# Expert outputs added up in DRAM by the scatter, and a tail that reads two sums per token instead of eight rows

## The reference

```
h2      = rmsnorm(x1) * (1 + sc2) + sh2
scores  = sigmoid(h2 @ w_router);  idx = top_8(scores + b_router) of 64 experts
wts     = 2.5 * scores[idx] / sum(scores[idx])
routed  = sum over the 8 experts e of a token:
              wts_e * ((silu(h2 @ w_gate_e) * (h2 @ w_up_e)) @ w_down_e)      # 1024 -> 256 -> 1024
shared  = (silu(h2 @ w_gate_s) * (h2 @ w_up_s)) @ w_down_s
x       = x1 + g2 * (routed + shared)
y       = rmsnorm(x, final_norm_w)
```

## Time and profile before

| | |
|---|---|
| median of three runs | 1163.04 us |
| the profiled execution | 1161.44 us |
| its span | 1159.7 us |
| PE busy | 932.3 us (80%) |
| DVE busy | 302.9 us (26%) |
| ACT, POOL busy | 169.5 us, 92.6 us |
| moved by DMA | 308.15 MB |
| expert loop, first gate/up to last scatter | 542 to 1094 us |
| tail behind the last scatter | 1098 us to the end |

### The profile page before, as it was taken

One profiled execution on the slowest core, in us unless ns is written; L12 is line 12 of the kernel. 1 busy time (PEld: TensorE's weight loads), 2 busy tenths in 40 slices (PEclk: granted clock), 3 DMA queues, 4 the chain that ended last, 5 costly groups with the idle time before them and its releaser, 6 DMA issues. The chain is left out here.

```text
span 1159.7 us, 12591 instructions
## 1 busy us (share of the span) xinstructions
PE 932.3 (80%) x4843; PEld 476.4 (41%) x4843; DVE 302.9 (26%) x560; ACT 169.5 (15%) x277; POOL 92.6 (8%) x162
## 2 busy tenths in 40 slices
PE   2699999999966999686999798987879778897500
PEld 0355567865511577433443333422334233332200
DVE  1507630560001321630212121211212112121057
ACT  0212511121000001201111111111111111111100
POOL 1000000000000000000111111211102112111000
PEclk9799999999986999797999998988999989899855
DMA  7822333113379240178699999999999999998390
GB/s 292 271 61 86 107 109 109 37 37 109 103 305 371 73 163 1 55 325 351 259 420 419 422 411 396 410 389 418 395 409 401 388 404 404 405 411 336 113 418 37
DMA packets 77389, 308.15 MB, mean 266 GB/s; under 512 B 10024, under 2 KB 38740, under 8 KB 49040
## 3 DMA queue, kind: packets, MB, share of 16 engines
q1 hardware_dynamic: 63120, 277.36, 60.8%
q0 software_dynamic: 10368, 25.18, 5.6%
q10 hardware_dynamic: 3840, 4.78, 1.2%
HBM read 297.33 MB, written 22.54 MB: 276 GB/s over the span
## 5 line engine op out<-in xcount | busy, mean ns | idle before, releaser
L450 PE MATMUL bank<-arena 128*32 128x512 f32 (+2 forms) x1536 | 277.8, 640 | 51.7 <-issue 50.9
L1393 PE MATMUL bank<-arena 128*128 128x384 f32 x640 | 208.3, 488 | 0.0
L450 PEld LDWEIGHTS bank<-arena 128*32 128x32 f32 (+2 forms) x1536 | 94.1, 131 | 233.0 <-issue 233.0
L1393 PEld LDWEIGHTS bank<-arena 128*128 128x128 f32 x640 | 122.1, 191 | 86.1 <-issue 2.3
L479 PE MATMUL bank<-arena 128*32 128x512 f32 (+2 forms) x768 | 130.9, 596 | 0.6 <-issue 0.6
L464 DVE TENSOR_TENSOR arena<-arena,bank 128x256 f32<-128x256 f32 x36 | 21.6, 599 | 229.7 <-ACT arena L461 229.7
L1378 PE MATMUL bank<-arena 128*2 128x512 f32 x192 | 34.2, 824 | 42.2 <-ACTq L1222 21.4
L479 PEld LDWEIGHTS bank<-arena 128*32 128x32 f32 (+2 forms) x768 | 39.4, 123 | 66.0 <-issue 66.0
L461 ACT ACTIVATE arena<-bank 128x256 f32<-128x256 f32 x36 | 22.1, 615 | 302.7 <-PE bank L450 302.7
L424 POOL DMA_INDIRECT arena<-h_rows,arena x36 | 37.4, 1038 | 314.4 <-DVE arena L418 236.3
L484 DVE TENSOR_SCALAR arena<-bank,arena 128x512 f32<-128x512 f32 x36 | 27.0, 751 | 105.3 <-PE bank L479 105.3
(11 more groups left out here) (228 smaller groups left out, 668.8 us busy)
## 6 DMA issues: line engine op xcount, KB each, us to landing
arena<-in_w_gate_e_dram SPq DMA_DIRECT2D x64, 1024.0 KB, 15.2
arena<-in_w_up_e_dram SPq DMA_DIRECT2D x64, 1024.0 KB, 29.5
arena<-in_w_down_e_dram SPq DMA_DIRECT2D x64, 1024.0 KB, 30.6
arena<-in_w_mod_dram SPq DMA_DIRECT2D x24, 1024.0 KB, 10.4
arena<-in_w_in_dram SPq DMA_DIRECT2D x22, 1024.0 KB, 5.3
arena<-expert_rows SPq DMA_DIRECT2D x3, 4096.0 KB, 21.6
arena<-in_w_out_dram SPq DMA_DIRECT2D x4, 1024.0 KB, 5.9
arena<-in_x_sample_dram ACTq DMA_DIRECT2D x2, 1024.0 KB, 15.6
```

The source lines that it names most:

```text
L450: ins = pe.matmul(bank[off:off + width, :], x_T[:, k, off:off + width], w[:, :, k, :], start=(k == 0), stop=(k == KT - 1))
L1393: ins = pe.matmul(ps[:, 0:TOK], w[:, k, P * (n % 2):P * (n % 2) + P], hT[:, k, :], start=(k == 0), stop=(k == KT - 1))
```

## The change

The scatter no longer writes each result to a row of its own. It adds it to one of two sums per token in DRAM (`expert_sums`, 768 rows of 4 KB, 3 MB): the first expert of a pass adds to sum 0, the second to sum 1, so that no row stands twice within a scatter. The parts:

1. The scatter carries `compute_op=ALU.add` (L433 in the new numbering), and scatter(i) waits until scatter(i-1) has landed. The first one waits for the zeroing.
2. ACT zeroes the sums with one 3 MB store from a zeroed tile (L1274), behind its first activations; DVE waits for it before it overwrites that tile.
3. `vals` has three values instead of four, and the running sums for the rank fall away. The row number in the sums is the token's number plus 0 or 384, by the partition (`far`, made once at the start).
4. In passes 4, 5 and 6 DVE computes `y_shared * g2` and adds it to `x1` (two operations on 128x1024 each).
5. The tail reads 1 MB per tile (two sums). DVE does three operations of 128x1024 per tile instead of six with 128x4096 and 128x2048 among them; the normalization of a tile comes behind the sums of the next one; ACT loads the Sqrt table before the tail.

```diff
-    rows_dram = nc.dram_tensor("expert_rows", [TOK * TOPK, D], F32).ap()
+    sums_dram = nc.dram_tensor("expert_sums", [2 * TOK, D], F32).ap()
...
-        def row_numbers(dve, b):
-            dve.tensor_tensor(rows_i[:, b, :], banks[7][:, 1:3], far, ALU.add)
-            return dve.tensor_copy(wt[:, b:b + 1], banks[7][:, 3:4])
+        def layout_of(quad):
+            return 0 if len(quad) == 1 else 1 if quad[0][2] == 96 else 2
+
+        def row_numbers(dve, b, layout):
+            dve.tensor_tensor(rows_i[:, b, :], banks[7][:, 1:2].to_broadcast([P, 2]), far[:, layout, :], ALU.add)
+            return dve.tensor_copy(wt[:, b:b + 1], banks[7][:, 2:3])
...
         def scatter_rows(pool, x, g, b):
             pool.sem_inc(x["rows_seen"], 1)
-            pool.indirect_dma_start(out=rows_dram,
+            pool.indirect_dma_start(out=sums_dram,
                                     out_offset=bass.IndirectOffsetOnAxis(ap=rows_i[:, g, 1:2], axis=0),
                                     in_=y_e[b], in_offset=None,
-                                    bounds_check=bound["scatter"], oob_is_err=False).then_inc(x["scattered"][b], 16)
+                                    bounds_check=bound["scatter"], oob_is_err=False, compute_op=ALU.add).then_inc(x["scattered"][b], 16)
...
             def scatter(i):
                 pool.wait_ge(x["y_a"], i + 1)
                 pool.wait_ge(x["y_b"], i + 1)
+                if i:
+                    pool.wait_ge(x["scattered"][(i - 1) % 2], 16 * ((i - 1) // 2 + 1))
+                else:
+                    pool.wait_ge(S["acc_zeroed"], 16)
                 scatter_rows(pool, x, i % 4, i % 2)
...
                 weighted_a(dve, i % 2, i % 4).then_inc(x["y_a"], 1)
+                if i in (4, 5, 6):
+                    link(dve.tensor_tensor(y_shared[:, i - 4, :], y_shared[:, i - 4, :], g2_rows[:, SEQ_OF[i - 4], :], ALU.mult))
+                    link(dve.tensor_tensor(x1[:, i - 4, :], x1[:, i - 4, :], y_shared[:, i - 4, :], ALU.add))
...
+                    if h == 0:
+                        dve.wait_ge(S["acc_zeroed"], 16)
...
             for t in range(NT):
-                ins = dve.tensor_tensor_scan(rank[:, t, :], ones[:, 0:NE], chosen[:, t, :], 0.0, ALU.mult, ALU.add)
-            link(ins)
-            link(dve.tensor_tensor(rank, rank, chosen, ALU.subtract))
...
-            for t in range(NT):
-                dve.wait_ge(rows_in_sem[t], 16)
-                r = rows_all[:, t]
-                link(dve.tensor_tensor(r[:, 0:4, :], r[:, 0:4, :], r[:, 4:8, :], ALU.add))
-                link(dve.tensor_tensor(r[:, 0:2, :], r[:, 0:2, :], r[:, 2:4, :], ALU.add))
+            def joined(t):
+                dve.wait_ge(sums_in_sem[t], 16)
+                r = sums_in[:, t]
                 link(dve.tensor_tensor(r[:, 0, :], r[:, 0, :], r[:, 1, :], ALU.add))
-                link(dve.tensor_tensor(r[:, 0, :], r[:, 0, :], y_shared[:, t, :], ALU.add))
                 link(dve.tensor_tensor(r[:, 0, :], r[:, 0, :], g2_rows[:, SEQ_OF[t], :], ALU.mult))
                 link(dve.tensor_tensor(x1[:, t, :], x1[:, t, :], r[:, 0, :], ALU.add))
                 dve.sem_inc(S["routed_ready"], 1)
+
+            def normed(t):
                 dve.wait_ge(S["final_sq"], t + 1)
...
+            for t in range(NT):
+                joined(t)
+                if t:
+                    normed(t - 1)
+            normed(NT - 1)
...
-            full_rows = rows_dram.rearrange("(t p k) d -> t p k d", p=P, k=TOPK)
-            for t in range(NT):
-                sp.dma_start(rows_all[:, t], full_rows[t]).then_inc(rows_in_sem[t], 16)
+            full_sums = sums_dram.rearrange("(m t p) d -> t p m d", m=2, p=P)
+            for t in range(NT):
+                sp.dma_start(sums_in[:, t], full_sums[t]).then_inc(sums_in_sem[t], 16)
...
             act.sem_inc(S["log_ready"], 1)
+            act.dma_start(sums_dram.rearrange("(r p) d -> p r d", p=P),
+                          at(a_st, D).unsqueeze(1).to_broadcast([P, 2 * NT, D])).then_inc(S["acc_zeroed"], 16)
...
+            act.activation(stat2[:, 15:16], ones[:, 0:1], ACT.Sqrt)
             for t in range(NT):
-                act.wait_ge(S["routed_ready"], 2 * t + 1)
+                act.wait_ge(S["routed_ready"], t + 1)
```

More of the change, by code:

```diff
@@ L236, in score_tile @@
             return at(a_x + 3 * NE * n, NT, NE)
-        scores, biased, rest, chosen, rank = (score_tile(n) for n in range(5))
+        scores, biased, rest, chosen = (score_tile(n) for n in range(4))
         top8 = at(a_x + 3 * NE * 5, NT, 8)
@@ L253, in program @@
         mod_rows = at(a_rows, 3, 512)
-        vals = at(a_rows, NT, NE, 4)
+        vals = at(a_rows, NT, NE, 3)
         onehot = at(a_rows + 768, 2, NT, ROWS)
@@ L274, in program @@
         actT_e = at(a_z + 1280, DE)
-        qv = at(a_z + 1536, 2, 2, NT, 4)
+        qv = at(a_z + 1536, 2, 2, NT, 3)
         order_i = at(a_z + 1584, NE).bitcast(I32)
@@ L286, in program @@
         part_f = at(take(1), 1)
-        far = at(take(2), 2)
+        far = at(take(6), 3, 2)
         most_f = at(take(1), 1)
         most_i = at(take(1), 1).bitcast(I32)
-        tok_far = at(take(2 * NT), 2, NT)
+        tok_far = at(take(NT), NT)
         before = arena[:, take(64):top[0]].bitcast(BF16)
@@ L359, in unit_view @@
             return v.rearrange("p (k n) -> p k n", k=KT)
-        rows_all = arena[:, 0:NT * TOPK * D].rearrange("p (t k d) -> p t k d", t=NT, k=TOPK)
-        rows_in_sem = [sem(f"rows_in{t}") for t in range(NT)]
+        sums_in = arena[:, 0:2 * NT * D].rearrange("p (t m d) -> p t m d", t=NT, m=2)
+        sums_in_sem = [sem(f"sums_in{t}") for t in range(NT)]
         ex_names = ("picked onehot_done tab_done rows_ready rows_seen xtr_done xT_a xT_b gu_done sil_done act_done "
@@ L503, in pool_experts @@
             bound["gather"] = pool.to_reg(TOK - 1)
-            bound["scatter"] = pool.to_reg(TOK * TOPK - 1)
+            bound["scatter"] = pool.to_reg(2 * TOK - 1)
             pool.wait_ge(S["order_ready"], 1)
@@ L611, in act_experts, with dve_experts @@
                 weighted_b(act, i % 2, i % 4).then_inc(x["y_b"], 1)
-        def dve_experts(dve, x):
+        def dve_experts(dve, x, link):
             def one_hot(i):
@@ L625, in numbers @@
                     dve.wait_ge(x["scattered"][i % 2], 16 * (i // 2 - 1))
-                row_numbers(dve, i % 4).then_inc(x["rows_ready"], 1)
+                row_numbers(dve, i % 4, layout_of(QUADS[i])).then_inc(x["rows_ready"], 1)
             def x_half(i):
@@ L724, in dve_spill @@
                 dve.wait_ge(x["tab_done"], n + 1)
-                row_numbers(dve, 0).then_inc(x["rows_ready"], 1)
+                row_numbers(dve, 0, 0).then_inc(x["rows_ready"], 1)
                 dve.wait_ge(x["xtr_done"], n + 1)
@@ L751, in vector_part_a @@
             link(dve.tensor_copy(iota1, iota_i))
-            link(dve.memset(far[:, 0:1], FAR))
-            link(dve.memset(far[:, 1:2], TOPK * FAR))
+            link(dve.memset(far.rearrange("p a b -> p (a b)"), FAR))
+            for layout, edge in ((1, 96.0), (2, 64.0)):
+                link(dve.tensor_scalar(far[:, layout, 1:2], part_f, edge, float(TOK), ALU.is_ge, ALU.mult))
+                link(dve.tensor_scalar(far[:, layout, 1:2], far[:, layout, 1:2], FAR, None, ALU.add))
             for t in range(NT):
-                dve.tensor_scalar(tok_far[:, 0, t:t + 1], part_f, float(P * t) - FAR, None, ALU.add)
-                link(dve.tensor_scalar(tok_far[:, 1, t:t + 1], part_f, float(P * t) - FAR, float(TOPK), ALU.add, ALU.mult))
+                link(dve.tensor_scalar(tok_far[:, t:t + 1], part_f, float(P * t) - FAR, None, ALU.add))
             link(dve.tensor_reduce(eye32, ident.rearrange("p (q r) -> p r q", r=32), AX.X, ALU.add))
@@ L1051, in vector_part_b @@
             for t in range(NT):
-                ins = dve.tensor_tensor_scan(rank[:, t, :], ones[:, 0:NE], chosen[:, t, :], 0.0, ALU.mult, ALU.add)
-            link(ins)
-            link(dve.tensor_tensor(rank, rank, chosen, ALU.subtract))
-            for t in range(NT):
-                dve.tensor_scalar(vals[:, t, :, 1], ones[:, 0:NE], tok_far[:, 0, t:t + 1], None, ALU.mult)
-                dve.tensor_scalar(vals[:, t, :, 2], rank[:, t, :], tok_far[:, 1, t:t + 1], None, ALU.add)
-            link(dve.scalar_tensor_tensor(out=vals[:, :, :, 3], in0=scores, scalar=ROUTED_SCALE,
+                dve.tensor_scalar(vals[:, t, :, 1], ones[:, 0:NE], tok_far[:, t:t + 1], None, ALU.mult)
+            link(dve.scalar_tensor_tensor(out=vals[:, :, :, 2], in0=scores, scalar=ROUTED_SCALE,
                                           in1=weight_sum.unsqueeze(2).to_broadcast([P, NT, NE]),
@@ L1110, in vector_part_b @@
                 dve.sem_inc(S["routed_ready"], 1)
+            def normed(t):
                 dve.wait_ge(S["final_sq"], t + 1)
                 link(dve.tensor_scalar(stat[:, t:t + 1], stat2[:, t:t + 1], 1.0 / D, EPS, ALU.mult, ALU.add))
```

(2 more changed lines are left out.)

8 lines of the change are left out of this document (4 added, 4 removed).

## The result

The changed kernel takes 1172.14 us (median of four runs, 1170.93 to 1175.59) against 1162.03 before on the same chip: a ratio of 1.0088, 95% interval 1.0057 to 1.0118. It is slower by 10 us (0.9%). Forecast was 1156, 0.5% faster. The profiled execution took 1171.46 us, its span is 1169.7.

The account below looks back on a forecast made before the run. The prediction took a DVE-bound tail and a DMA-bound middle of the loop as the limits. Its terms, -36.1 + 28 + 1.5 = -6.6 us, gave 1156 us after adjusting to the runs' median, with a range of 1128 to 1196.

Parts of the forecast that it names:

- What bounds the kernel: Whole kernel: a tail that hangs on DVE, and a stretch from 580 to 1060 us bound by DMA bytes.
- The tail, -36.1: From SP's read-back to the end: 61.3 us before, 25.2 after, so 36.1 us saved.
- The scatter's bytes, +28: In the saturated stretch the addition's extra read takes the place of weight bytes, costing 28 us.
- Its first half: At the scatter: an addition has to read the destination too, 12.58 MB more.
- Its price two ways: Extra read in the saturated stretch: 27.5 us by bytes at 407 GB/s, 28.9 us by the queue's share.
- The wait, 0: On POOL, waiting for the scatter before costs 0; its landing was estimated at 11 to 14 us.
- The last scatter, +1.5: At the loop's end the scatter runs alone, 3.6 us before; the added read was taken as 1.5 us.
- What costs nothing: Zeroing store, two DVE operations in passes 4 to 6, dropped running sums: no cost; Sqrt load already in the tail.
- the hidden read: Rival in the saturated stretch: the addition's read is free, 1127 us, or half free, 1142; chance 0.24.
- the chain: Rival in the loop: scatters stand one landing time apart, 67 us more in place of 28, 1195 us; chance 0.14.
- an addition at three times a row's price: Rival at the scatter: the extra is 56 us, time 1184; chance 0.26 together with scatters waiting on each other.
- the total stays: DMA engines move 424 GB/s without scatters, 420 with: a scattered byte takes the place of a weight byte.

Follow-up runs that it names:

- e1: The changed kernel with the addition left out: the scatter overwrites, the wait and zeroing stay. 1127.29 us, ratio 0.9686.
- e2: The changed kernel without the addition, each pass issuing a second plain scatter of the same rows to a second table. 1173.20 us.
- e3: The kernel before, its scatter to 3072 rows of their own adding instead of writing, no wait between scatters. 1205.84 us.
- e8: The kernel before with the filled places dealt out over the groups of partitions that one DMA engine serves. 1146.20 us, ratio 0.9854.
- e7: The changed kernel with the filled places dealt out over the groups of partitions that one DMA engine serves. 1146.40 us, ratio 0.9845.
- e10: The changed kernel with places spread over engine groups and, for one large expert, towards engines that small experts leave free. 1136.18 us, ratio 0.9765.
- e11: The kernel before with the places dealt evenly over groups of 8 neighbouring partitions. 1169.25 us, ratio 1.0051.
- e5: The changed kernel without the addition, plus a direct store of all 128 rows per pass, 18.9 MB in all. 1169.94 us.

## Why the prediction was wrong, by its own steps

- **What bounds the kernel**: right. The tail and the saturated stretch are the two places; e1 separates them.
- **The tail, -36.1**: right, -35.7. The first load landed in 4.8 us (4.9 taken); three operations of 1.24 us a tile, with about 0.1 us more behind each tile; ACT's square lay hidden, since DVE waited only 0.33 us for the root. The store took 3.1.
- **The scatter's bytes, +28**: this is the step that failed. Its first half held: the addition is one more transfer (e1, e2, e3). Its price did not. "Its price two ways" took 11.18 MB by the mean rate and by the queue's mean share, and both ways divide the load evenly over 16 engines. The loop waits for the most loaded one, which has 288 rows where the mean is 192, so 28 has to be taken 288/192 = 1.5 times: 42. Measured are 43.0 at the last scatter's start, of which e1, without the addition, has 1.7 (its last scatter starts at 1095.37), so 41.3 for the addition.
- **The wait, 0**: right. e1 keeps it, and POOL never waited for it. The landing of 10.3 us is below the estimate of 11 to 14.
- **The last scatter, +1.5**: 2.7. A lone adding scatter lands after 6.0 us instead of 3.6 (below).
- **What costs nothing**: right within the 1.7 us of e1. The zeroing store raised the DMA share from 100 to 120 us from 0.34 to 0.70, and PE stayed at 20.00 of 20:

```profile
100.00:120.00 20.00, 20.00 (x64) 11.79 (x63) 19.64 (x19) 0.98 (x2) 0.00 (x0) 1.00 0.70 259
```

- In pass 4 the two new operations of DVE ran at 610.75 and 612.00, and the one-hot behind them at 613.86, ahead of the look-up.
- **The rivals**: the hidden read is out (e1), the chain is out, and an addition at three times a row's price (56 us) is as far from the measured 41.3 as 28 is, and is no mechanism: the addition is two transfers (e2), both dear. The range of 1128 to 1196 held the time, but by its width alone: it reached so far up for a chain that did not come. The side was wrong.

The rows could have shown it. With scatter and gather the rate was 420 in the stretch picked for the earlier trace rows, against 424 without, and from that "the total stays" was read. Over the whole stretch it is 407. The prediction names the missing part as a reason for the hidden read, as time that may be free; all of it but the 4 GB/s between 424 and 420 was the uneven load, which makes a transfer dearer. The 20 us picked lie early in the loop: of the 40 slices on the page of the kernel before, those from 580 to 667 us show 419 to 422 GB/s, and those from there to 1044 us 388 to 418. From 640 to 1040 us, before and then e8:

```profile
640.00:1040.00 400.00, 338.69 (x2116) 141.82 (x2110) 68.66 (x174) 58.47 (x103) 59.98 (x96) 0.94 1.00 404
```

```profile
640.00:1040.00 400.00, 346.31 (x2178) 144.88 (x2171) 70.99 (x180) 59.97 (x105) 61.36 (x99) 0.95 1.02 420
```

With the places spread, the 420 of the early stretch hold to the end of the loop.

All of the extra read shows in the share and none of it in the bytes. The queue of the gathers and scatters, after and then in e1:

```profile
q0 software_dynamic: 10368, 25.19, 8.5%
```

```profile
q0 software_dynamic: 10368, 25.18, 5.8%
```

Packets and MB are the same with and without the addition, but the time of the packets is 8.5% of 1169.7 us, 99 us, instead of 65. One by one: in e1 a packet of 4 KB (one row) takes 159 ns in the median; after, the same 6144 packets fall into two halves, one at 159 and one at 327 ns. So an adding packet takes twice a plain one's time, and the mean of the added time over 16 engines is about the 28 to 33 us that the prediction had; the rest of the 41 is the uneven load.

The Trainium skill, Collectives: The Full Stack, section "The bandwidth ceiling: the fold count and why AG ≠ RS ≠ AR", has the adding step of a ring at half the rate of a copy, because the addition needs two source reads; the runs here agree, 327 ns against 159 for a packet, and e1 and e2 with 44.8 us against 45.9. The Trainium skill, DMA: Bandwidth & Descriptors, section "The descriptor swizzle", gives each engine four neighbouring partitions and the four that lie 32 further for a transfer of 128 partitions. The places of e7 to e10 follow that grouping, and together with e11 they bear it out for indirect transfers too.

## What to carry to other kernels

Where a stream of loads keeps the DMA engines full, price a further transfer by the rows of its most loaded engine, not by its bytes: a gather or scatter whose empty places lie together costs as if they were filled. Spread the filled places over the groups of partitions that one engine serves; here that alone is 17 us of 1163 with no byte less. An addition in DRAM is a second transfer of the same rows: move it into a full stream only if it saves more than that elsewhere, and compare it with mending the part it is meant to shorten.

## What the runs showed of the hardware that was not expected

- **A DMA share of 1.00 does not say that all engines are at work all the time.** It was 1.00 from 580 to 1060 us in before, after, e2, e5 and e8 alike, with rates from 376 to 414 GB/s. The rate beside the best stretch without scatters, 424, says more.
- **The read of an adding transfer is in no count of bytes**, so GB/s falls where nothing got slower but the work per byte.
- **An adding scatter is dearer on GpSimd**: 1.60 us of issue instead of 1.01, and one copy behind it (L403) takes 757 ns in the median, where it takes 200 before and 201 in e1. DVE's one-hot comes later for it, but PE's look-up still starts right behind gate and up (630.09 us in one pass, where gate and up end at 630.16), so it cost nothing here. The rows of e7 and then e8, where all 64 copies stand together:

```profile
L405 POOL COPY arena<-arena 128x9 f32 x64 | 29.4, 702 | 2.6 <-issue 2.6
```

```profile
L405 POOL COPY arena<-arena 128x12 f32 x64 | 11.3, 197 | 3.3 <-issue 3.1
```

- **A lone adding scatter lands 2.4 us later** than a plain one. All 36 of the kernel after, against the earlier trace rows:

```profile
L433 POOL DMA_INDIRECT expert_sums<-arena x36: 1552/1596/1760, 559.1 to 1136.6; - x36
...
DMA to landing us min/median/max: 6.0/10.3/11.4
```
